# A two-layer transformer trunk: loads moved across the seams between stages, keys projected first, the last combination on three engines

## The reference, cut to what matters

```python
for i in range(2):
    sh1, sc1, g1, sh2, sc2, g2 = split(silu(c) @ ada_w[i] + ada_b[i], 6)      # conditioning; the same for ctx
    h = rmsnorm(x, norm1_g[i]) * (1 + sc1) + sh1
    q, k, v = split(h @ wqkv); q, k = rope(rmsnorm(q)), rope(rmsnorm(k))
    x = x + g1 * (attend(q, k, v) @ wo)
    h2 = rmsnorm(x, norm2_g[i]) * (1 + sc2) + sh2
    y = moe(h2)                  # per token w0 * expert_a(h2) + w1 * expert_b(h2)
    x = x + g2 * y
```

## Time and profile before

| | |
|---|---|
| time of three runs, median (lowest to highest) | 3275.97 us (3274.22 to 3279.16) |
| the profiled execution: its time, its span | 3273.99 us, 3272.2 us |
| busy: PE, DVE, ACT, POOL | 2900.0 us (89%), 1303.3 us (40%), 782.2 us (24%), 675.3 us (21%) |
| mean granted TensorE clock | 0.944 |
| DMA | 734.38 MB, mean 224 GB/s |

### The profile page before, as it was taken

One profiled execution on the slowest core, in us unless ns is written; L12 is line 12 of the kernel. 1 busy time (PEld: TensorE's weight loads), 2 busy tenths in 40 slices (PEclk: granted clock), 3 DMA queues, 4 the chain that ended last, 5 costly groups with the idle time before them and its releaser, 6 DMA issues. The chain is left out here.

```text
span 3272.2 us, 34525 instructions
## 1 busy us (share of the span) xinstructions
PE 2900.0 (89%) x13041; PEld 1614.4 (49%) x13041; DVE 1303.3 (40%) x2294; ACT 782.2 (24%) x1755; POOL 675.3 (21%) x927
## 2 busy tenths in 40 slices
PE   7999988999999948999999859959999589999991
PEld 3444334888884533444444324448875334443330
DVE  4544202988882252111111165359972421111114
ACT  2211102777771000000000043136641000000000
POOL 2555200555552110000000035400002110000000
PEclk9999999999999958999999979979999689999996
DMA  6334576242413248999999383153322399999975
GB/s 248 101 96 136 194 247 190 49 97 49 97 53 119 97 191 333 413 385 414 388 405 392 136 304 121 51 142 66 66 66 97 138 411 427 426 427 427 428 336 215
DMA packets 205156, 734.38 MB, mean 224 GB/s; under 512 B 29376, under 2 KB 124784, under 8 KB 168896
## 3 DMA queue, kind: packets, MB, share of 16 engines
q1 hardware_dynamic: 104656, 632.80, 51.6%
q10 hardware_dynamic: 85040, 61.60, 5.8%
q0 software_dynamic: 15296, 37.78, 2.9%
HBM read 662.32 MB, written 87.62 MB: 229 GB/s over the span
## 5 line engine op out<-in xcount | busy, mean ns | idle before, releaser
L1688 PE MATMUL psum<-moe_ring,moe_xT 128*64 128x512 f32 (+1 forms) x2240 | 709.9, 604 | 14.5 <-DMA moe_ring<-in_e_w 12.3
L382 PE MATMUL psum<-qkv_w,act_hT 128*128 128x512 f32 x1376 | 612.5, 598 | 0.1
L1688 PEld LDWEIGHTS psum<-moe_ring,moe_xT 128*64 128x64 f32 (+1 forms) x2240 | 276.2, 163 | 412.3 <-issue 410.1
L382 PEld LDWEIGHTS psum<-qkv_w,act_hT 128*128 128x128 f32 x1376 | 257.3, 192 | 308.2 <-issue 308.1
L1709 PE MATMUL psum<-moe_ring,moe_hT 128*64 128x512 f32 (+1 forms) x1120 | 352.8, 594 | 1.6 <-DVE moe_hT L1789 1.6
L1785 DVE TENSOR_TENSOR moe_hh<-psum,moe_sg 128x512 f32<-128x512 f32 x50 | 34.6, 692 | 669.3 <-PE psum L1688 669.3
L1246 PE MATMUL psum<-wo,out_oT 128*128 128x512 f32 x576 | 255.7, 599 | 1.4 <-DVEq L1262 1.0
L1709 PEld LDWEIGHTS psum<-moe_ring,moe_hT 128*64 128x64 f32 (+1 forms) x1120 | 133.1, 160 | 184.6 <-issue 180.4
L994 DVE TENSOR_REDUCE att_nmax<-psum 128x1 f32<-128x1280 f32 (+1 forms) x160 | 204.0, 1276 | 29.2 <-PE psum L887 28.2
L887 PE MATMUL psum<-att_kT,att_q 128*128 128x512 f32 (+1 forms) x832 | 198.1, 370 | 10.2 <-ACTq L135 5.1
L950 ACT ACTIVATE att_prob<-psum,att_nmax 128x1280 f32<-128x1280 f32 (+1 forms) x160 | 185.1, 1157 | 57.2 <-DVE att_nmax L994 53.7
(11 more groups left out here) (250 smaller groups left out, 3280.1 us busy)
## 6 DMA issues: line engine op xcount, KB each, us to landing
moe_ring<-in_e_w SPq DMA_DIRECT2D x216, 2048.0 KB, 16.2
ada_w<-in_ada_w SPq DMA_DIRECT2D x48, 1024.0 KB, 6.4
qk_d<-qkv_stg ACTq DMA_DIRECT2D x112, 256.0 KB, 2.5
att_q<-qk_d SPq DMA_DIRECT2D x32, 640.0 KB, 14.2
att_q<-qk_d SPq DMA_DIRECT2D x64, 256.0 KB, 5.0
qkv_w<-in_a_wqkv SPq DMA_DIRECT2D x6, 2048.0 KB, 9.2
att_kT<-qk_d SPq DMA_DIRECT2D x32, 320.0 KB, 5.7
prep_y<-y_d SPq DMA_DIRECT2D x10, 1024.0 KB, 6.5
```

Source lines behind the costliest of these rows:

```text
L382: ins = nc.tensor.matmul(psum[:, u.par, :], hT[:, k, u.t * P:(u.t + 1) * P], qw[:, u.C % 2, k], start=(k == 0), stop=(k == KD - 1))
L1688: ins = nc.tensor.matmul(psum[part, bank, :], xT[:, 4 * half + k, part], ring[:, w13[x, half] % RING, k, bank * DE:(bank + 1) * DE], start ...
```

## The change

- Layer 0, front: the eight loads of head 0, which SP issued in one go after `load_ada(24)`, are issued one at a time after `load_ada` of 28, 30, ..., 42. The 16 small loads of ACT, which all stood at step 12, are spread: six at step 12, then one at each step up to 22.
- Seam from the experts of layer 0 to the second front: x of tiles 0 and 1 and both g2 rows are loaded before the barrier (`sp_ahead`), behind the last fallback weights; after it SP starts with y of tiles 0 and 1. For this x has its own buffers (`tail_x`). The sums of squares and their roots, `pss` and `prs`, are fixed tensors now.
- Layer 1, front: the kv chunk comes first (ten tiles), then the two q chunks.
- Seam to the second attention: the keys are loaded when the kv chunk is stored, and q of tile 0, first half, when its unit is stored, both before the barrier.
- Last stage: all x tiles and g2 are loaded ahead, before the barrier; y alone behind it. ACT does u = w0 y0, DVE u += w1 y1 and u *= g2, and the last addition is done by POOL for even tiles and by DVE for odd ones. The loop is written out and its copy of the two weights is gone.

```diff
     def load_x(sp, l, t):
         if l:
-            src = xs_d[t * P:(t + 1) * P, :]
             if t >= 2:
                 sp.wait_ge(s_pu, t - 1)
-            sp.dma_start(py2[:, t % 2], y_d[...]...).then_inc(s_px[t % 2], 16)
+            sp.dma_start(pxt1[:, t % 2], xs_d[t * P:(t + 1) * P, :]).then_inc(s_px[t % 2], 16)
...
+    def sp_ahead(sp, l):
+        sp.wait_ge(s_fbtab, l + 1)
+        if l == 0:
+            for t in range(2):
+                load_x(sp, 1, t)
+            for s in range(2):
+                sp.dma_start(pg2[:, s], mod_d[0, s:s + 1, 5 * D:].broadcast_to([P, D])).then_inc(s_pg, 16)
+        else:
+            last_ahead(sp)
...
             for n in range(11, 48):
                 load_ada(sp, n)
-                if n == 24:
+                if n == 28:
                     sp.wait_ge(s_qev, 42)
                     for par in range(2):
                         sp.wait_ge(s_qst[par], 16 + 32 * 20)
-                    load_head(sp, 0)
+                if n >= 28 and n % 2 == 0 and (n - 28) // 2 < 8:
+                    load_head(sp, 0, (n - 28) // 2)
             return
...
         load_qkv(sp, l, 2)
+        for par in range(2):
+            sp.wait_ge(s_pst[par], 16 * (TA // 2))
+            sp.wait_ge(s_qst[par], 16 + 32 * 25)
+        sp_att1_keys(sp)
+        sp.wait_ge(s_qst[0], 16 + 32 * 26)
+        load_q(sp, 0, 0)
...
-                                  [("qk", 8, 0, TX), ("qk", 8, 0, TX), ("kv", 4, 1, TA)]]):
+                                  [("kv", 4, 1, TA), ("qk", 8, 0, TX), ("qk", 8, 0, TX)]]):
...
+    def act_last(act):
+        for t in range(TX):
+            act.wait_ge(s_fyin[t % 4], 16 * (t // 4 + 1))
+            nc.scalar.activation(fu[:, t], fy[:, t % 4, 0], ACT.Copy, scale=wsel[:, 0, t:t + 1]).then_inc(s_fw, 1)
+            if t >= 2:
+                store_out(act, t - 2)
...
     def dve_last(dve):
         dve.wait_ge(s_fg, 16)
+        for t in range(TX):
+            dve.wait_ge(s_fw, t + 1)
+            u = fu[:, t]
+            dvec.link(dve, nc.vector.scalar_tensor_tensor(u, fy[:, t % 4, 1], wsel[:, 1, t:t + 1], u, ALU.mult, ALU.add))
+            nc.vector.tensor_tensor(u, u, fg[:, :], ALU.mult).then_inc(s_fm, 1)
+            if t % 2:
...
+                nc.vector.tensor_tensor(u, last_x(t), u, ALU.add).then_inc(s_fx, 1)
+
+    def pool_last(pool):
...
+        for t in range(0, TX, 2):
+            pool.wait_ge(s_fm, t + 1)
+            nc.gpsimd.tensor_tensor(fu[:, t], last_x(t), fu[:, t], ALU.add).then_inc(s_fxp, 1)
```

More of the change, by code:

```diff
@@ L247, in build, with __init__ @@
     class Unit:
-        def __init__(self, l, n, chunk, t, kind, heads, which):
-            self.n, self.chunk, self.t, self.kind, self.heads, self.which = n, chunk, t, kind, heads, which
+        def __init__(self, l, n, chunk, t, kind, heads, which, part):
+            self.n, self.chunk, self.t, self.kind, self.heads, self.which, self.part = n, chunk, t, kind, heads, which, part
             self.U = n + 60 * l
@@ L255, in __init__, with part_of @@
             self.par = n % 2
+    def part_of(l, chunk):
+        return chunk if l == 0 else [2, 0, 1][chunk]
     UNIT = [[], []]
     for l, sections in enumerate([[("qk", 8, 0, TA), ("qk", 8, 0, TA), ("qk", 8, 1, TA), ("qk", 8, 1, TA), ("v", 0, 0, TA), ("v", 0, 0, TA)],
-                                  [("qk", 8, 0, TX), ("qk", 8, 0, TX), ("kv", 4, 1, TA)]]):
+                                  [("kv", 4, 1, TA), ("qk", 8, 0, TX), ("qk", 8, 0, TX)]]):
         for chunk, (kind, heads, which, nt) in enumerate(sections):
             for t in range(nt):
-                UNIT[l].append(Unit(l, len(UNIT[l]), chunk, t, kind, heads, which))
+                UNIT[l].append(Unit(l, len(UNIT[l]), chunk, t, kind, heads, which, part_of(l, chunk)))
     FIRST_V = 40
@@ L377, in product @@
                     pe.wait_ge(s_ptd, u.t + 1)
-            elif l and u.chunk == 2:
-                pe.wait_ge(s_pta, 2 * TA)
             pe.wait_ge(s_qaccfree, u.U + 1)
@@ L475, in square @@
                 act.wait_ge(s_pu, t + 1)
-            nc.scalar.activation(psq[:, t % 2], (pu if l else pxt)[:, t % 2], ACT.Square, scale=1 / 32, accum_out=pss[:, t % 2:t % 2 + 1]).then_inc(s_pss, 1)
+            nc.scalar.activation(psq[:, t % 2], (pu if l else pxt0)[:, t % 2], ACT.Square, scale=1 / 32, accum_out=pss[:, t % 2:t % 2 + 1]).then_inc(s_pss, 1)
             if l:
@@ L496, in evac @@
             for part in range(2):
-                act.dma_start(qk_d[4 * u.chunk:4 * u.chunk + nb, part, :, u.t * P:(u.t + 1) * P].rearrange("h p n -> p h n"), qstg[:, u.par, part, 0:nb].bitcast(F32)).then_inc(s_qst[u.par], 16)
+                act.dma_start(qk_d[4 * u.part:4 * u.part + nb, part, :, u.t * P:(u.t + 1) * P].rearrange("h p n -> p h n"), qstg[:, u.par, part, 0:nb].bitcast(F32)).then_inc(s_qst[u.par], 16)
         def take(u):
@@ L813, in full_before, with load_head @@
         return n // TA * TX + min(n % TA, TX)
-    def load_head(sp, h):
+    def load_head(sp, h, only=None):
         buf = (h + 1) % 2
@@ L819, in load_head @@
             for m in range(2):
[L820 removed]
+                if only in (None, 2 * part + m):
+                    sp.dma_start(kT[buf][64 * part:64 * part + 64, m].bitcast(F32), qk_d[KD + h, part, 64 * m:64 * m + 64, :]).then_inc(s_kq[buf], 16)
         for rows in range(2):
             for m in range(2):
[L823 removed]
+                if only in (None, 4 + 2 * rows + m):
+                    sp.dma_start(aq0[buf][64 * rows:64 * rows + 64, m].bitcast(F32), qk_d[h, :, 64 * m:64 * m + 64, :].rearrange("x d n -> d x n")).then_inc(s_kq[buf], 16)
     def sp_att0(sp):
@@ L1923, in dve_fallback @@
         fallback_loop(dve, l, body)
-    s_fin = [sem(f"s_fin{n}") for n in range(4)]
-    s_fx, s_fst, s_fg = sem("s_fx"), [sem(f"s_fst{n}") for n in range(4)], sem("s_fg")
+    s_fin, s_fyin = [sem("s_fin0"), sem("s_fin1")], [sem(f"s_fyin{n}") for n in range(4)]
+    s_fw, s_fm, s_fx, s_fxp, s_fg = sem("s_fw"), sem("s_fm"), sem("s_fx"), sem("s_fxp"), sem("s_fg")
+    s_fst = sem("s_fst")
     A = Arena("last")
-    fx = A("x", [P, 4, D])
     fy = A("y", [P, 4, 2, D])
-    fu = A("u", [P, 4, D])
@@ L1931, in build @@
[L1931 to L1944 removed]
+    fu = A("u", [P, TX, D])
@@ new lines, in build, with last_x, last_ahead @@
+    fxb = nc.alloc_sbuf_tensor_at("last_xb", [P, 5, D], F32, offset=arena0_at + 6 * 4 * D * 4)
+    def last_x(t):
+        return fxa[:, t] if t < 3 else fxb[:, t - 3]
+    def last_ahead(sp):
+        for t in range(3):
+            sp.dma_start(fxa[:, t], xs_d[t * P:(t + 1) * P, :]).then_inc(s_fin[0], 16)
+        sp.dma_start(fg[:, :], mod_d[1, 0:1, 5 * D:].broadcast_to([P, D])).then_inc(s_fg, 16)
+        sp.wait_ge(s_used, used_by(1, len(UNITS[1]) - 1, "down"))
+        for t in range(3, TX):
+            sp.dma_start(fxb[:, t - 3], xs_d[t * P:(t + 1) * P, :]).then_inc(s_fin[1], 16)
@@ L1946, in dve_last, with store_out @@
+    def store_out(act, t):
+        if t % 2:
+            act.wait_ge(s_fx, t // 2 + 1)
+        else:
+            act.wait_ge(s_fxp, t // 2 + 1)
+        act.dma_start(out[0, t * P:(t + 1) * P, :], fu[:, t]).then_inc(s_fst, 16)
     def dve_last(dve):
         dve.wait_ge(s_fg, 16)
-        def body(i):
-            for n in range(4):
-                dve.wait_ge(s_fin[n], 32 * (i + 1))
-                dve_combine(dve, 4 * i + n, fx[:, n], fy[:, n], fu[:, n], fw[:, n % 2], fg[:, :]).then_inc(s_fx, 1)
```

109 lines of the change are left out of this document (48 added, 61 removed).

## The result

| | before | changed |
|---|---|---|
| median of the runs (lowest to highest) | 3275.09 us of 4 (3273.12 to 3279.16) | 3217.43 us of 4 (3215.75 to 3219.42) |
| ratio | | 0.9824, 95% interval 0.9812 to 0.9836 |
| the profiled execution: span | 3272.2 us | 3214.7 us |
| busy PE, DVE, ACT, POOL | 2900.0, 1303.3, 782.2, 675.3 us | 2896.9, 1299.6, 792.7, 689.5 us |
| mean granted clock | 0.944 | 0.951 |

The sum had come to 3214.5 for a profiled execution (this one: 3216.31) and to 3216 for the median. Busy times hardly moved; the 57.5 us of the spans are idle time and slow stretches. To see which, I cut both spans at fixed instructions. Product n is the start of the n-th group of eight contraction steps in PE's timeline, one row x16 (60 in the first layer, 26 in the second); the barriers are read at the first instruction behind them.

What follows compares the result with a forecast made beforehand. PE, busy 89% of 3272.2 us, was taken as the bound, with five places of waiting or slowness: 7.9 + 13.3 + 12.3 + 14.6 + 11.4 = 59.5 us off, 3214.5 profiled, 3216 us median; range 3205 to 3230.

Steps and rivals of the forecast that it cites:

- The sum: Five gains over the whole kernel, 59.5 us together, giving 3214.5 us for a profiled execution.
- Small loads: Step 12, first layer: spreading ACT's 16 loads removes PE's wait and slow transposes and product, 7.9 us.
- head 0: Between conditioning weights: spreading eight loads removes PE's wait for ada_w and the slow rows behind it, 13.3 us.
- The rival in which the pieces are not hidden: Loads between conditioning weights still make PE wait, 18 us of waits, 3234 us; chance 6%.
- The seam into the second front: Start of second projection: first product 8.6 us earlier, shorter rounds with kv units first 3.7 us; 12.3 us together.
- tile 2 lands near 1898: Second projection's start: third tile arrives then, so combine(2) starts near 1899.3, 8.7 us earlier.
- that rival (3225): Second front: tile 2 comes as late as before, the 8.6 us stay, only shorter rounds count; chance 14%.
- The seam into the second attention: First score's 19.9 us wait for keys goes; 2.2 us for later units and 3.1 for the tail return; net 14.6.
- The last stage: Final eight tiles: DVE needs 34.5 us instead of 43.6 and starts 2.3 us earlier, 11.4 us gained.
- The rival of the free overlap: Last stage: POOL's additions don't hold DVE, 8.8 us more gained, 3207 us; chance 12%.
- What I had at nothing: Matrix products, experts and their ring, outside the five places: expected as before, 0 us.
- The signs: Expected profile: no early PE bracket over 1 us, products 11.0 us apart, four DVE rows near 3.4, end some 45 us after barrier.

Runs made afterwards that it cites:

- small_batch: Changed kernel with all 16 small loads of ACT issued at step 12 again: 3224.23 us.
- head_batch: Changed kernel with the eight loads of head 0 issued in one go behind weight load 28: 3229.39 us.
- head_dense: Changed kernel with one load of head 0 behind every weight load from 28 to 35, not every second: 3228.41 us.
- low_first: Changed kernel with one line moved: in the second projection DVE does low of unit s-2 ahead of combine of tile s+3: 3201.63 us.
- q_first: Changed kernel with keys and first half of q of tile 0 loaded behind the barrier, and units in the old order q, q, keys: 3236.93 us.
- seam_behind: Changed kernel with x of tiles 0 and 1 and both g2 rows loaded behind the barrier into the second projection: 3222.30 us.
- best_pe: Changed kernel with low ahead of combine, even last additions on PE with own PSUM banks, eight y buffers, and later stores by ACT: 3196.79 us.
- last_dve: Changed kernel with all eight last additions on DVE and none on POOL: 3212.06 us.
- again: The changed kernel itself, unaltered, measured again on the same chip as later experiments: 3216.25 us.

## Why the prediction was right, and where its terms were off

**Small loads** (7.9; measured 8.0, or 6.7 by the slowest of the other profiles) and **head 0** (13.3; measured 13.4): right, and `small_batch` and `head_batch` lose 7.5 and 13.7 us when each is undone. The rival in which the pieces are not hidden has fallen, but `head_dense` shows how near it stood: twice the density costs 7.5 us.

**The seam into the second front** (8.6 + 3.7; measured 6.0 + 4.3). The step that failed is "tile 2 lands near 1898": it landed 2.6 us later. From `weigh(0)` on I had 4.7 MB at 406 GB/s. It was 5.24 MB, since ACT stores tile 0 (0.52 MB, 1.3 us) at the moment at which tile 2 is issued, and they took 14.0 us, which is 375 GB/s. `combine(0)` was where I put it, 6.15 for 6.0. For the rounds the size was near, in part by luck. I had `mean` and `low` in the ring for their own 0.27 us each, so 0.53 us shorter rounds for seven tiles. The rows have it otherwise: the second, third and fourth round are 1.8, 1.3 and 1.2 us shorter than before, the first is 1.4 longer, and the later four lie between 0.1 longer and 0.8 shorter. And `low` matters more by its place than by its length: `low_first` takes 3.1 us off a round.

I had also added the two parts of this seam as if they were independent, and they are not. From the barrier to the ninth product it is 116.2 us before; 112.8 with the early loads alone (`q_first`), so they give 3.4 there; 111.9 with the keys first alone (`seam_behind`); and 104.6 to 106.1 with both, so behind the keys the same loads give 5.9 to 7.4. In the old order part of the head's gain is given back in the rounds. In the changed kernel it is not, and that rival (3225) has fallen.

**The seam into the second attention** (19.9 - 3.1 = 16.8, and 2.2 against it; measured 15.6 and 2.2). The 19.9 us are gone to the last 0.03. The tail of the last unit is 4.2 us longer, not 3.1: 20.07 us from the last product to the barrier where it was 15.84. Up to the issue of its store it lost 3.3 us, as forecast; the store itself, of twice the bytes, takes 3.33 us to the barrier where it took 2.44, and I had not counted it. The fifth unit of the attention did not wait.

**The last stage** (11.4; measured 14.3). The step that was mis-sized is DVE's work: it is 32.85 us and I had 34.5. Each addition on POOL lengthened one DVE row by 2.03 us, not 2.2, so 8.1 instead of 8.8; without them 20 such instructions take 24.8 (`best_pe`), not 25.7, since an instruction that waits for nothing of the one before starts 0.1 us before that one's row ends. The start was 2.7 us earlier (2.3 forecast), and the way from DVE's last row to the end 0.8 us shorter, which I had left alone. The rival of the free overlap has fallen twice, by the rows and by `last_dve`.

What held the four additions is read from the rows. POOL's addition starts at 3181.29 while DVE's instruction of 3181.03 runs; it ends 2.20 us after that one's end (3182.31 to 3184.51), so it stood for 1.02 us and then took its 2.20. DVE's next instruction starts at 3182.34 and ends 1.08 us after POOL's end. Each waits for the whole of the other. The Trainium skill, page "SBUF — State Buffer", section "Who interferes with whom", calls it an exclusive lock, with the other side fully blocked; the trace agrees, with 2.20 us held of 2.35. As advice the number is this: an addition of 1.23 us moved from DVE to POOL cost DVE 2.03 us.

**What I had at nothing.** From the first score to the last barrier the changed kernel shows 1.0 us more than before. It is all in the first two units of the attention: PE's rows are at the lower clock until 2126 to 2128, 14 us behind the first score, and before for 11 us (at 2124.20 a row of 16 takes 1.98 us, and at 2168.32, as far behind its own first score, it took 1.10). But it isn't a loss of the change: in `again`, the same kernel, the clock is up 12.3 us behind the first score and the whole stretch is 1057.45 us, 1.1 less than before. Over all kernels here the stretch lies between 1057.3 and 1059.6 us, and product 60 to the barrier, with its 0.6 us, between 1343.9 and 1347.2. What sets the moment at which the clock rises stays open.

**The signs.** Four DVE rows of 3.25 us stand beside POOL's additions (near 3.4 forecast), no bracket <-DMA ada_w came back, and the first score waits for the barrier alone. Products are 11.08 us apart (11.0). Between 120 and 540 us PE has brackets over 1 us, but all from 529.70 on, where the attention of layer 0 starts; the first, 5.12 us, is its barrier, which took 5.14 before as well. The end is 42.2 us behind the last barrier, not 45.

Term by term the gains missed by +0.1, +0.1, -2.6, +0.6, -1.2 and +2.9 us, and by -1.9 for what I had at nothing (0.3 at the start, 0.6 between product 60 and the barrier, 1.0 here): -2.0 in all. That the total lies 1.4 us from 3216 is in part their cancelling, and 1.4 us is also what the changed kernel's gain differs by between its two comparisons.
